# Two norms of a hybrid encoder block computed in another form: the latent norms by products with ones, the MLP norm behind its first product

## What is computed

```python
def rms_norm(x, g, eps=NORM_EPS):
    y = x * lax.rsqrt(jnp.mean(x * x, axis=-1, keepdims=True) + eps)
    return y * g

proj = rms_norm(h, mix_norm) @ w_in
c_q, c_kv, k_rope = cols[:192], cols[192:320], cols[320:352]      # of proj
q  = rms_norm(c_q, q_norm) @ w_uq
kv = rms_norm(c_kv, kv_norm) @ w_ukv
... # rotary keys, chunk-causal attention of 8 heads; beside it the RWKV-7 group
h = h + concat([att, rw]) @ w_out
h = h + mem_cross_attention(rms_norm(h, ca_norm), mem_n, ca_wq, ca_wkv, ca_wo)
h = h + jnp.square(jax.nn.relu(rms_norm(h, mlp_norm) @ w_up)) @ w_down   # w_up 1024 x 4096
out = rms_norm(h, final_norm)
```

## Time and profile before

| | us |
|---|---|
| median of 3 runs | 2168.03 (2166.11 to 2168.35) |
| the profiled execution, whole | 2170.02 |
| its span (first to last instruction) | 2168.1 |
| PE busy | 1966.4 (91% of the span) |
| DVE, ACT, POOL busy | 779.7, 436.5, 477.6 |
| mean granted TensorE clock | 0.945 |

### The profile page before, as it was taken

How to read it: one execution, slowest core, us unless ns; L and a number is a source line. 1 busy time by engine, 2 the same in 40 slices (tenths; PEclk the granted TensorE clock), 3 DMA queues, 4 the chain that set the end, 5 groups by cost and what they waited for, 6 DMA issues and landing times.

```text
span 2168.1 us, 25863 instructions
## 1 busy us (share of the span) xinstructions
PE 1966.4 (91%) x10096; PEld 1540.0 (71%) x10096; DVE 779.7 (36%) x1101; ACT 436.5 (20%) x785; POOL 477.6 (22%) x283
## 2 busy tenths in 40 slices
PE   5999999988989898858889988979999999999996
PEld 4866666645676667637787755868888888888885
DVE  6532323244646464444361053352112212211233
ACT  3122222242313232231031121021001101101100
POOL 2210212011201010012103220324334333333430
PEclk9999998987989999968999989989999999999998
DMA  5010010002030202022132000101111111111111
GB/s 201 29 30 18 20 37 10 8 14 61 21 76 16 65 16 53 1 84 82 46 109 78 29 20 10 48 20 48 49 48 48 48 48 48 48 48 48 48 48 78
DMA packets 76356, 100.86 MB, mean 47 GB/s; under 512 B 28928, under 2 KB 56064, under 8 KB 76032
## 3 DMA queue, kind: packets, MB, share of 16 engines
q1 hardware_dynamic: 76288, 99.90, 14.7%
HBM read 86.76 MB, written 13.12 MB: 46 GB/s over the span
## 4 chain that ended last, share of the span: by engine, by line
PE 83%; DVE 10%; ACT 3%; issue 2%; DMA 1%; POOL 0%; SPq 0%; DVEq 0%; ACTq 0%; POOLq 0%
PE PS L690 46%; PE PS L731 7%; PE PS L831 3%; PE PS L860 3%; PE PS L888 2%; PE PS L845 2%; PE PS L1259 2%; PE PS L1075 1%; PE PS L885 1%; DVE tmp L1646 1%; PE PS L1196 1%; PE PS L1039 1%; PE PS L797 1%; PE PS L937 1%; PE PS L795 1%
## 5 line engine op out<-in xcount | busy, mean ns | idle before, releaser
L690 PE MATMUL PS<-xn,wsp 128*128 128x512 f32 x2880 | 664.6, 393 | 16.7 <-DVE xn L1639 13.7
L690 PEld LDWEIGHTS PS<-xn,wsp 128*128 128x128 f32 x2880 | 544.9, 190 | 135.6 <-issue 11.6
L690 PE MATMUL PS<-hid,wsp 128*128 128x512 f32 x1536 | 348.8, 389 | 0.0
L576 POOL CAST wsp<-wraw 128x1024 fp32r<-128x1024 f32 x104 | 110.1, 1059 | 1019.9 <-PE PS L690 696.3
L690 PEld LDWEIGHTS PS<-hid,wsp 128*128 128x128 f32 x1536 | 288.4, 188 | 59.8
L578 POOL TENSOR_TENSOR wsp<-wraw,wsp 128x1024 fp32r<-128x1024 f32 x104 | 282.7, 2719 | 8.3
L731 PE MATMUL PS<-xn,wsp 128*128 128x512 f32 x576 | 150.6, 409 | 4.2 <-DVE proj L1689 4.2
L731 PEld LDWEIGHTS PS<-xn,wsp 128*128 128x128 f32 x576 | 107.4, 194 | 36.0 <-issue 15.1
L1610 ACT ACTIVATE tmp<-PS 128x1024 f32<-128x1024 f32 x32 | 32.8, 1026 | 494.2 <-PE PS L690 494.2
L2172 DVE TENSOR_TENSOR tmp<-tmp 128x1024 f32<-128x1024 f32 x32 | 39.2, 1225 | 211.7 <-ACT tmp L1610 211.7
L2187 DVE TENSOR_TENSOR H<-PS,H 128x1024 f32 x24 | 29.4, 1224 | 218.6 <-PE PS L690 218.6
(11 more groups left out here) (273 smaller groups left out, 2319.6 us busy)
## 6 DMA issues: line engine op xcount, KB each, us to landing
wraw<-in_weights_dram SPq DMA_DIRECT2D x120, 512.0 KB, 3.5
H<-in_x_dram SPq DMA_DIRECT2D x16, 512.0 KB, 6.8
H<-x_dram SPq DMA_DIRECT2D x32, 128.0 KB, 2.6
H<-xt_dram SPq DMA_DIRECT2D x32, 128.0 KB, 2.7
out_dram<-proj SPq DMA_DIRECT2D x8, 512.0 KB, 3.6
a_dram<-H SPq DMA_DIRECT2D x12, 256.0 KB, 2.3
o_dram<-o_stage SPq DMA_DIRECT2D x3, 512.0 KB, 2.7
ssum<-in_head_weights_dram SPq DMA_DIRECT2D x4, 320.0 KB, 4.3
```

Source lines behind the costliest of these rows:

```text
L576: nc.gpsimd.tensor_copy(wsp[:, k, :, 0, :], raw).then_inc(w_head, 1)
L690: last = nc.tensor.matmul(PS[:, 2 * k + half, :], wsp[:, k, kt, a, :], src[:, kt, b, HALF * half:HALF * half + HALF], start=(kt == 0 and ( ...
```

## The change

It has two parts.

Latent norms: PE multiplies the squares with a 128 x 128 matrix of ones (one column of constants, broadcast), 512 columns at a time: 2 products for the key (banks 0 and 1) and 4 for the query (banks 4 and 5). Each result holds the sum on every partition at once. ACT takes the logarithm with scale and epsilon, then exp of -0.5 times it, over 128 x 1024 for each of the two, into `mP[0]` and `mQ`. The sums with one column, the 1/sqrt on 128 x 16 and both spreads are gone. DVE scales `T_CKV` first, and all three scalings now read the factor from SBUF. PE waits for the key's logarithm ahead of the rotary products (which write bank 0), and head 0 for `cq1` in place of `ckv`.

MLP norm: the factor is left out of the input of the up units. They now read `hid`, which holds `H` times the gain, made tile by tile while the units of U_O come out. The factor (positive, one for each position) is multiplied into the ReLU's result by DVE, ahead of the square. The hidden tiles go to `xn`. PE does the sum's 8 products behind the first up unit and the spread's 8 behind the second; DVE copies the spread factor to `ssum`. Spreads now use banks 4 and 5.

```diff
@@ tensor
-            for w in range(NW):
-                nc.tensor.matmul(PS[:, 4, w:w + 1], mQ[:, win(w)], con[:, C_ONE:C_ONE + 1], start=True, stop=False)
...
+            ones = con[:, C_ONE:C_ONE + 1].broadcast_to([P, P])
+            for half in range(2):
+                hs = slice(HALF * half, HALF * half + HALF)
+                last = nc.tensor.matmul(PS[:, half, :], ones, mP[0][:, hs], start=True, stop=True)
+            last.then_inc(MP_PE.sem, MP_PE.one("skv"))
...
+                nc.tensor.matmul(PS[:, 4 + half, :], ones, mQ[:, hs], start=True, stop=False)
+                last = nc.tensor.matmul(PS[:, 4 + half, :], con[0:HD, C_ONE:C_ONE + 1].broadcast_to([HD, P]),
+                                        mK[0:HD, hs], start=False, stop=True)
...
+            pe.wait_ge(MP_ACT.sem, MP_ACT.at("lkv", -1))
...
-            pe.wait_ge(MP_DVE.sem, MP_DVE.at("rstd", -1))
-            for w in range(NW):
-                last = nc.tensor.matmul(PS[:, 4 + w // 4, P * (w % 4):P * (w % 4) + P],
-                                        small[:, 32 + w:33 + w].broadcast_to([P, P]), ident, start=True, stop=True)
...
-                    m_at(MP_DVE, "ckv")
+                    m_at(MP_DVE, "cq1")
...
+            up(0, 0, 0)
+            norm_sum(2)
+            up(0, 0, 1)
+            norm_spread(2)
@@ scalar
-            act.wait_ge(MP_DVE.sem, MP_DVE.at("var", -1))
-            nc.scalar.activation(small[:, 16:32], small[:, 0:16], ACT.Sqrt).then_inc(MP_ACT.sem, MP_ACT.one("std"))
+            latent_factor(0, "kv", KVR, mP[0])
+            latent_factor(4, "q", QR, mQ)
+            for name, dst in (("kv", mP[0]), ("q", mQ)):
+                act.wait_ge(MP_ACT.sem, MP_ACT.at(f"l{name}", -1))
+                nc.scalar.activation(dst, dst, ACT.Exp, scale=-0.5).then_inc(MP_ACT.sem, MP_ACT.one(f"f{name}"))
...
+            for kt in range(KT):
+                act.wait_ge(h_added, KT + kt + 1)
+                nc.scalar.activation(hid[:, kt, 0, :], H[:, kt, :], ACT.Copy, scale=vec[:, V_MLP + kt:V_MLP + kt + 1]).then_inc(
+                    head_ready, 1)
+                act.wait_ge(sq_added, 2 * KT + kt - 1)
+                square(kt % 2, H[:, kt, :])
@@ vector
-            mp(nc.vector.reciprocal(small[:, 32:48], small[:, 16:32]), "rstd")
+            dve.wait_ge(MP_ACT.sem, MP_ACT.at("fkv", -1))
+            mp(nc.vector.scalar_tensor_tensor(proj[:, T_CKV, :], proj[:, T_CKV, :], vec[:, V_KVN:V_KVN + 1], mP[0],
+                                              ALU.mult, ALU.mult), "ckv")
...
-            norm(2)
-            scale_and_split(2, 3, V_MLP)
...
+                    nc.vector.scalar_tensor_tensor(both[:, 1, :], tile, vec[:, bass.ds(j + V_MLP, 1)],
+                                                   both[:, 0, :].bitcast(F32), ALU.mult, ALU.subtract).then_inc(xn_ready, 1)
...
+                nc.vector.tensor_tensor(tmp[:, k, :], tmp[:, k, :], ssum[:, :], ALU.mult).then_inc(relu_scaled, 1)
+                dve.wait_ge(relu_scaled, n + (k + 1))
+                nc.vector.tensor_tensor(tmp[:, k, :], tmp[:, k, :], tmp[:, k, :], ALU.mult).then_inc(hsq_ready, 1)
```

More of the change, by code:

```diff
@@ L1275, in _, with up, down @@
             gemm(U_O, 8, xn, ca_ready)
[L1276 to L1279 removed]
+            def up(c, i, k):
+                unit(16 * c + 2 * i + (U_MLP + k), k, hid, split_ready(3))
+            def down(c):
                 with pe.Fori(0, 4) as i:
                     for k in range(2):
[L1282 removed]
+                        unit(16 * c + 2 * i + (U_MLP + 8 + k), k, xn,
+                             lambda kt: pe.wait_ge(hid_ready, 8 * c + kt + 3))
+            up(0, 0, 0)
+            norm_sum(2)
+            up(0, 0, 1)
+            norm_spread(2)
+            with pe.Fori(1, 4) as i:
+                for k in range(2):
+                    up(0, i, k)
+            down(0)
+            with pe.Fori(1, 4) as c:
                 with pe.Fori(0, 4) as i:
                     for k in range(2):
[L1285 to L1286 removed]
+                        up(c, i, k)
+                down(c)
             norm(3)
@@ L2181, in _ @@
-            with dve.Fori(0, 3) as c:
-                hidden(c)
+            nc.vector.memset(ssum[:, :], 0.0).then_inc(ssum_zero, 1)
+            dve.wait_ge(ssum_zero, 2)
+            with dve.Fori(0, 4) as i:
+                for k in range(2):
+                    j = 2 * i + k
+                    tile = H[:, bass.ds(j, 1), :].rearrange("p a t -> p (a t)")
+                    dve.wait_ge(acc_ready, 2 * i + (U_O + k + 3))
+                    nc.vector.tensor_tensor(tile, two(2 * k), tile, ALU.add).then_inc(h_added, 1)
+                    dve.wait_ge(h_added, 2 * i + (8 + k + 1))
+                    nc.vector.sem_inc(acc_free, 1)
+                    both = hid[:, bass.ds(j, 1), :, :].rearrange("p a b t -> p (a b) t")
+                    dve.wait_ge(head_ready, 2 * i + (3 * KT + k + 1))
+                    nc.vector.scalar_tensor_tensor(both[:, 1, :], tile, vec[:, bass.ds(j + V_MLP, 1)],
+                                                   both[:, 0, :].bitcast(F32), ALU.mult, ALU.subtract).then_inc(xn_ready, 1)
+                    dve.wait_ge(sq_ready, 2 * i + (2 * KT + k + 1))
+                    dve.wait_ge(sq_added, 2 * i + (2 * KT + k))
+                    nc.vector.tensor_tensor(ssum[:, :], ssum[:, :], tmp[:, k, :], ALU.add).then_inc(sq_added, 1)
@@ L2189, in _, with hiddens @@
                         nc.vector.sem_inc(acc_free, 1)
-            hidden(3)
+            def hiddens(c, i0):
+                with dve.Fori(i0, 4) as i:
+                    for k in range(2):
+                        hidden(c, i, k)
+            norm(2)
+            for k in range(2):
+                dve.wait_ge(relu_ready, k + 1)
+                nc.vector.sem_inc(acc_free, 1)
+            dve.wait_ge(nb_ready, 3)
+            nc.vector.tensor_copy(ssum[:, :], two(4)).then_inc(factor_made, 1)
+            dve.wait_ge(factor_made, 1)
+            for k in range(2):
+                hidden(0, 0, k, True)
+            hiddens(0, 1)
+            downs(0)
+            with dve.Fori(1, 3) as c:
+                hiddens(c, 0)
+                downs(c)
+            hiddens(3, 0)
             residual(UNITS - 8, 40, 3)
```

125 lines of the change are left out of this document (60 added, 65 removed).

## The result

The changed kernel takes 2134.78 us (median of 4 executions, 2131.77 to 2136.66), the kernel before it 2167.07 us in the same comparison (4 executions, 2161.12 to 2168.35). The ratio is 0.9854, with a 95% interval of 0.9835 to 0.9872: 32.3 us gained, where 27.0 were forecast. The direction was right.

A forecast was written before the change was run, and what follows sets the result against it. PE sets the end: the latent norms are PE time, the MLP norm a stall. Gains of 7.4 and 19.6 us sum to 27.0, taking the median 2168.03 to 2141.0 us; own range 2138 to 2145, 8-in-10 range 2137 to 2148.5.

The forecast's parts named there:

- 27.0 were forecast: Whole kernel: gain of 27.0 us, 7.4 from the latent norms and 19.6 from the MLP norm.
- The direction: Whole kernel: the changed kernel was forecast to be faster, chance 0.95, with same 0.02 and slower 0.03.

## What to carry to other kernels

Before trusting the length of a stage, look at how long TensorE's clock was at half in it, and take the untouched stages' scatter into the range: here 0.4 us of time for each microsecond at half, up to 17 us in one stage. Compare edited stages with edited stages and not whole times, where a single execution can reverse the sign of a 4 us step. When a DVE pass with two SBUF inputs meets a GpSimd pass, price it as its own length plus what is left of the other, and keep the cover above that sum.

## What had not been expected of the hardware

The granted clock fell in some executions and not in others of one program, at the same instructions, with PE busy: in the latent norms 0 us and 6.8 us of half time in traces of the changed kernel, and 3.4 us in others with the same instructions there. And a wait costs more than its length: 19.2 us of waits at five places in the MLP, with 30 us more of half time, came to 33.2 us.
